# A relative-bias line stored 128 times, so that a strided transfer builds the strips without TensorE

## The chip, the cores and the metric

The kernel runs on one core of a Trainium2 chip. The metric is the device time of one execution in microseconds (us). The engines are TensorE (PE, with its weight loads as PEld), VectorE (DVE), ScalarE (ACT), GpSimd (POOL) and SyncE (SP), which here only issues DMA transfers.

## The reference, cut to what matters

Two model blocks in float32 run one after the other on 512 tokens of width 1024 (528 with 16 meta tokens in the first block). The first layer of the first block is the one that the change touches: a sparse attention with an index score that selects 128 keys for each query, and a relative-position bias for each head.

```
def rel_bucket(rel):            # rel = key position - query position; 32 buckets
    ...
def dsa_attention(q, k, v, iq, ik, iw, rel_bias, chunk, valid, topk):
    def block(i):               # 128 queries
        sc = relu(einsum('bqhd,bsd->bqhs', iqb, ik))
        score = einsum('bqhs,bqh->bqs', sc, iwb) * IDX_SCALE
        score = where(adm, score, NEG_INF)
        _, idx = lax.top_k(score, topk)
        logits = einsum('bqhd,bqkhd->bhqk', qb, kg) * dh ** -0.5
        bias = rel_bias[rel_bucket(idx - qpos)]
        logits = logits + transpose(bias)
        p = softmax(where(ok, logits, NEG_INF))
        return einsum('bhqk,bqkhd->bqhd', p, vg)
layer_ab: oa = dsa_attention(...) * silu(ag); ob = gla_chunked(...); out = concat(oa, ob) @ w_out
```

After it come a layer with retention and stick-breaking attention, and a second block with four feed-forward parts, a latent attention and a gated convolution.

## The kernel before

Activations stay in on-chip memory with the features on the partitions. All weights stream through in blocks of at most 1024 x 256 (1 MB): `load_block` (L436) asks for a block on SP's queue, `split_high` (L451, the activation at L459) rounds it on ACT to `wh`, `split_low` (L461, L466) makes the remainder `wl` on POOL, and PE makes three products for each tile (L486, L490 or L493, by form). There are two slots for a block: block b may be loaded when the low part of block b - 2 is made. The order on each engine is written out by hand in the five functions at the end (L2162 to L2341), and semaphores join them. PE's dense products are dealt out step by step between the small matmuls of attention stages.

The relative bias depends only on key minus query position, so the kernel makes one line for each head: a matmul of the bias table with a one-hot matrix gives `line`, 8 partitions (one for a head) x 655 values, which ACT copies out of PSUM (L2239, L2240). For 128 queries on the partitions the bias is then a strip: row p reads the line from position 127 - p on. SBUF rows can't be read at another offset for each partition, so the line goes to memory (`bias_line`, L2176) and comes back as `strip` (128 partitions x 8 heads x 528) with one transfer (L2181), in which row p starts at p. That is the wrong way round, and 16 matmuls with a reversed identity matrix (`flip`, `strips_pe`, L1641; the trace shows each as two) turn it, with 8 copies from PSUM on ACT (`strips_act`, L1647).

What stands around it:
- SP: store of the line, then the loads of further blocks, then the wait for the store (`bias_stored`) and for the end of the linear attention (`gla_mix_low`; the strips lie where its tiles lay), the transfer of the strips, the next blocks.
- ACT: `index_act` (L1504) begins with a wait for `bias_stored`, since `relu` lies where `line` lay. Ahead of it in ACT's order is the rounding of block 4. `index_act` makes the relu of the index scores (L1511) from matmuls at L1483; DVE adds them up (L1542, L1545). PE's first group of scores, two dense steps and the head weights (L1491) need no relu; every further group needs the relus of the group ahead of it.
- DVE then selects the keys by rounds of maximum and replace (L1586, L1587), the last ones alone before the softmax stage; L1589 and the memset at L1590 end each selection.
- The softmax stage (`soft_pe` L755, `soft_dve` L834, `soft_act` L898) has 40 steps of one head and one query tile: scores (L773), logits with bias (L852), maximum (L854), exponential (L910), turn (L785, L788), values (L804), and dense steps of the gate projection and the output projection as filling. In the first eight steps DVE reads `strip` itself (16 queries); from the ninth on POOL adds strip and selection mask ahead (L2208).

Of the kernel before, what the change touches and what calls it, by code (L numbers as in the profile page):

```python
# [5 lines left out]
F32 = mybir.dt.float32  # L6
# [3 lines left out]
ACT = mybir.ActivationFunctionType  # L10
AX = mybir.AxisListType

P = 128
# [4 lines left out]
T = SEQ + META  # L18
# [11 lines left out]
HEADS = 8  # L30
# [10 lines left out]
def token_tile(t):  # L41

    return (0, META) if t == 0 else (META + P * (t - 1), P)
# [54 lines left out]
BIAS_SPAN = T + P - 1  # L98
# [124 lines left out]
BLOCKS, FIRST, UNITS = weight_plan()  # L223


def units_before(b):
    return BLOCKS[b].unit0 if b < len(BLOCKS) else len(UNITS)


def evacs_before(b, engine):  # L230

    return sum(x[0] == engine for x in UNITS[:units_before(b)])
# [6 lines left out]
def program(nc, inp, const_in, buckets_in, out, bias_line):  # L239
# [3 lines left out]
    def S(name):  # L243

        if name not in sems:
            sems[name] = ctx.enter_context(nc.semaphore(name))
        return sems[name]


    ps = ctx.enter_context(nc.psum_tensor("ps", [P, 8, 512], F32))  # L250

    def at(name, off, shape, dtype=F32):

        assert off % 8 == 0
        return nc.alloc_sbuf_tensor_at(name, shape, dtype, offset=SBUF0 + 4 * off)
# [14 lines left out]
    def const(name, c0=0, n=None, rows=P):  # L270
        pack, at_, width = CONST[name]
        return K[pack][0:rows, at_ + c0:at_ + (width if n is None else c0 + n)]
# [9 lines left out]
    line = at("line", 33224, [HEADS, BIAS_SPAN])  # L282
# [35 lines left out]
    strip = at("strip", 37608, [P, HEADS, T])  # L318
# [102 lines left out]
    def banks(b0, width, rows=P):  # L421

        return ps[0:rows, b0:b0 + 2, 0:width // 2]

    def halves(ap, width):
        return ap.rearrange("p (a b) -> p a b", a=2) if len(ap.shape) == 2 else ap
# [968 lines left out]
    ag = [(AG + q, i) for q in range(2) for i in range(2)]  # L1395
# [34 lines left out]
    def dsa_between(eng, i):  # L1430

        for n, end in enumerate(DSA_ENDS):
# [3 lines left out]
            elif end == i - 1:  # L1436
                dsa_evict_dve(eng, n)

    dsa = Soft("dsa", [0, 1, 2, 3, 4],
               lambda h, c0, n: aqT[(h % 2) * HD:(h % 2) * HD + HD, h // 2, c0:c0 + n],  # L1440
               lambda h, c0, n: akT[(h % 2) * HD:(h % 2) * HD + HD, h // 2, c0:c0 + n],
               lambda kt, h: av[0:token_tile(kt)[1], kt, h * HD:(h + 1) * HD],
               lambda t: META + P * t, lambda t, n, h: rq[0:n, t:t + 1], None, 0, lg, pt, oa, mx, agT, 0, True, ((0,), (2,), 3, (4,), 7),
               None, dsa_between, oa_meta, lambda e: e.wait_ge(S("gate_silu"), 8))
# [20 lines left out]
    halfT = T // 2  # L1465
# [166 lines left out]
        nc.vector.scalar_tensor_tensor(out=halves(dst, T), in0=banks(bank_of(u), T, n), scalar=HD ** -0.5 if name == "bq" else 1.0,  # L1632
                                       in1=halves(rstd[0:n, :], T), op0=ALU.mult, op1=ALU.mult).then_inc(S("evac_dve"), 1)

    def strips_pe(pe):
        pe.wait_ge(S("side_in"), 32)
        for h in range(HEADS):
            if h >= 2:
                pe.wait_ge(S("strip_out"), h - 1)
            for x in range(2):  # L1640
                last = nc.tensor.matmul(ps[:, 2 + 2 * (h % 2) + x, 0:halfT], const("flip"), strip[:, h, x * halfT:(x + 1) * halfT], start=True, stop=True)  # L1641
            last.then_inc(S("strip_turned"), 1)

    def strips_act(act):
        for h in range(HEADS):
            act.wait_ge(S("strip_turned"), h + 1)
            nc.scalar.activation(halves(strip[:, h, :], T), banks(2 + 2 * (h % 2), T), ACT.Copy).then_inc(S("strip_out"), 1)  # L1647

    def cd_name(b):
        return [n for n in ("cq", "ck", "cv", "cg", "dk", "dq0", "dv0", "dg0", "dq1", "dv1", "dg1", "out_ret") if FIRST[n] <= b][-1]  # L1650

# [510 lines left out]
    @block.sync  # L2162
    def _(sp):
        sp.dma_start(xm[:, :], inp["meta_tokens"]).then_inc(S("const_in"), 16)
        sp.dma_start(K[0][:, :], const_in[0]).then_inc(S("const_in"), 16)
        load_block(sp, 0)
        for t in range(NT):
            sp.dma_start(xt[:, t, :], inp["x"][0, t * P:(t + 1) * P, :]).then_inc(S(f"x_in_{t}"), 16)
        load_block(sp, 1)
        sp.dma_start(onehot[:, :], buckets_in).then_inc(S("bias_in"), 16)  # L2170
        sp.dma_start(rb[:, :], inp["rel_bias"]).then_inc(S("bias_in"), 16)
        sp.dma_start(gate_w2[:, :], inp["gla_gate_w2"][0]).then_inc(S("side_in"), 16)
        for b in range(2, 4):
            load_block(sp, b)
        sp.wait_ge(S("bias_rows"), 2)
        sp.dma_start(bias_line, line[:, :]).then_inc(S("bias_stored"), 16)  # L2176
        for b in range(4, FIRST["ag"] + 1):
            load_block(sp, b)
        sp.wait_ge(S("bias_stored"), 16)
        sp.wait_ge(S("gla_mix_low"), NT + 1)  # L2180
        sp.dma_start(strip[:, :, :], bass.AP(bias_line.tensor, bias_line.offset, [[1, P], [BIAS_SPAN, HEADS], [1, T]])).then_inc(S("side_in"), 16)  # L2181
        for b in range(FIRST["ag"] + 1, C0 + 2):
            load_block(sp, b)
        sp.wait_ge(S("unit_done"), units_before(C0))
        sp.dma_start(K[1][:, :], const_in[1]).then_inc(S("side_in"), 16)
        sp.dma_start(K[3][:, :], const_in[3]).then_inc(S("side_in"), 16)
        for b in range(C0 + 2, FIRST["second"] + 2):
            load_block(sp, b)
        second_sp(sp)

    @block.gpsimd
    def _(pool):
        for b in range(OG + 1):
            split_low(pool, b)

        for i in range(HEADS, 5 * HEADS):
            t, h = dsa.steps[i]
            if i == HEADS:
                pool.wait_ge(S("strip_out"), HEADS)
            if h == 0:  # L2200
                pool.wait_ge(S("selected"), t)
            if i >= HEADS + 2:
                pool.wait_ge(S("dsa_logits"), i - 1)
            w = dsa.width(t)
            at_ = strip_at(t)
            if i == 3 * HEADS:
                pool.wait_ge(S("unit_done"), units_before(OG))
            nc.gpsimd.tensor_tensor(bm_of(i)[:, 0:w], strip[:, h, at_:at_ + w], score[:, SCO[t - 1]:SCO[t - 1] + w], ALU.add).then_inc(S("bias_masked"), 1)  # L2208
            if i in (9, 15, 23, 31):
                split_low(pool, OG + 1 + (9, 15, 23, 31).index(i))  # L2210
        for b in range(OG + 5, FIRST["second"]):
            split_low(pool, b)
        second_pool(pool)

    @block.scalar
    def _(act):
# [39 lines left out]
        lin_high(act, gla, NT)  # L2256
        for b, i in av_units[NT + 1:]:
            ab_act(act, b, i)
        strips_act(act)
        soft_act(act, dsa, lambda e: None)  # L2260
        for b in range(OG + 4, OG + 8):
            late_act(act, "cd", 2 * (b - OG - 4))
# [17 lines left out]
    def _(dve):  # L2280
# [37 lines left out]

        for _ in rounds:
            pass  # L2320
        soft_dve(dve, dsa, lambda e: e.wait_ge(S("strip_out"), HEADS))
        for b in range(OG + 4, OG + 8):
            add_out_dve(dve, b, True, "cd")
        late_scale_dve(dve, "cd")
# [17 lines left out]
    def _(pe):  # L2342
# [3 lines left out]
        for k in range(KT):  # L2346
            last = nc.tensor.transpose(ps[:, 4, k * META:(k + 1) * META], xm[:, k * P:(k + 1) * P], ident[0:META, 0:META])
# [3 lines left out]
        for g in range(2 * NT):  # L2351
# [8 lines left out]
            for k in range(4):  # L2360
                last = nc.tensor.transpose(ps[:, 4 + (g + 1) % 4, k * P:(k + 1) * P], xt[:, t, (k0 + k) * P:(k0 + k + 1) * P], ident)
# [35 lines left out]
        for _ in range(steps_in(av_units[NT + 1:])):  # L2397
            next(dense)
        pe.wait_ge(S("gla_gated"), NT + 1)
        strips_pe(pe)  # L2400
        pe.wait_ge(S("strip_out"), HEADS)

        def dsa_fill(i):
            if i == 6:
# [77 lines left out]
```

## Time and profile before

| | |
|---|---|
| median of the runs | 2760.39 us (2758.14 to 2762.59, 3 runs) |
| the profiled execution | 2754.39 us |
| its span, first to last instruction | 2752.6 us |
| mean granted clock of TensorE | 0.986 |
| PE / PEld busy | 95% / 78% |
| DVE / ACT / POOL busy | 38% / 32% / 39% |
| DMA, mean | 79 GB/s |

The profile is one execution. Busy shares are means over the whole span, in which many stages with different limits follow each other; the stages of this change are the first 300 us. A timeline row gives start, duration, engine, line, operation and tiles, and in brackets how long the engine was idle before it and what it waited for.

### The profile page before, as it was taken

The numbers are of one execution on the slowest core, as the hardware profiler recorded it, in microseconds if no ns is written. First come the engines' busy times: TensorE is split into PE (matmuls) and PEld (weight loads), VectorE is DVE, ScalarE is ACT, GpSimd is POOL, SyncE is SP. The second block draws the span as 40 slices with busy tenths as digits, with TensorE's granted clock in tenths as the row PEclk, the third lists the DMA queues.
The fourth block names the chain that finished last, engine by engine and source line by source line (L and its number), as shares of the span: only waits on it lengthen the run. The fifth ranks groups of instructions, "written<-read, shape, count | busy, mean of one in ns | idle before, by whom it ended". The sixth has DMA issues, their size and how long they took to land.

```text
span 2752.6 us, 32062 instructions
## 1 busy us (share of the span) xinstructions
PE 2623.4 (95%) x13245; PEld 2134.7 (78%) x13245; DVE 1033.9 (38%) x1742; ACT 881.1 (32%) x1289; POOL 1068.3 (39%) x830
## 2 busy tenths in 40 slices
PE   7999898999996999999789999999999999999999
PEld 6888787886655888877667888878888888888887
DVE  4655355224335312145554222243121444421212
ACT  4432333225543222232534222232222322322221
POOL 3232232331114444443204444444444444454443
PEclk9999999999998999999999999999999999999999
DMA  4122001220012233221102332233322232223322
GB/s 129 59 62 82 28 24 54 77 77 32 23 39 91 89 94 105 92 87 59 58 9 92 100 97 94 88 96 98 101 92 92 92 104 95 92 92 95 104 92 77
DMA packets 215851, 217.78 MB, mean 79 GB/s; under 512 B 10599, under 2 KB 213090, under 8 KB 215706
## 3 DMA queue, kind: packets, MB, share of 16 engines
q1 hardware_dynamic: 215504, 215.68, 24.5%
q8 instruction: 105, 1.72, 0.3%
q14 instruction: 40, 0.33, 0.0%
q10 hardware_dynamic: 202, 0.06, 0.0%
HBM read 213.60 MB, written 2.12 MB: 78 GB/s over the span
## 4 chain that ended last, share of the span: by engine, by line
PE 86%; DVE 5%; ACT 4%; issue 2%; POOL 2%; DMA 1%; ACTq 0%; DVEq 0%; SPq 0%
PE ps L490 65%; PE ps L486 7%; PE ps L493 3%; POOL wl L466 2%; PE ps L804 2%; PE ps L773 1%; ACT wh L459 1%; PE ps L2021 1%; PE ps L1999 1%; PE ps L788 1%; DVE score L1587 1%; PE ps L2415 1%; DVE top L1586 0%; PE ps L1483 0%; PE ps L1980 0%
## 5 line engine op out<-in xcount | busy, mean ns | idle before, releaser
L466 POOL TENSOR_TENSOR wl<-raw,wh 128x512 fp32r<-128x512 f32 x794 | 1039.6, 1340 | 1591.3 <-ACT wh L459 1591.3
L490 PE MATMUL ps<-NH,wh 128*128 128x512 f32 (+1 forms) x1824 | 720.8, 395 | 38.1 <-POOL wl L466 27.8
L490 PE MATMUL ps<-NL,wh 128*128 128x512 f32 (+1 forms) x1824 | 715.4, 392 | 0.0
L490 PE MATMUL ps<-NH,wl 128*128 128x512 f32 (+1 forms) x1824 | 714.8, 392 | 0.0
L459 ACT ACTIVATE wh<-raw 128x2048 fp32r<-128x2048 f32 (+4 forms) x219 | 380.3, 1737 | 459.9 <-PE ps L490 413.6
L490 PEld LDWEIGHTS ps<-NH,wh 128*128 128x128 f32 (+1 forms) x1824 | 344.9, 189 | 119.9 <-POOL wl L466 30.9
L490 PEld LDWEIGHTS ps<-NH,wl 128*128 128x128 f32 (+1 forms) x1824 | 344.7, 189 | 74.3
L490 PEld LDWEIGHTS ps<-NL,wh 128*128 128x128 f32 (+1 forms) x1824 | 344.9, 189 | 73.6 <-issue 1.4
L490 PE MATMUL ps<-GH,wh 128*128 128x512 f32 x832 | 330.0, 397 | 3.0 <-DVE GL L728 2.3
L490 PE MATMUL ps<-GH,wl 128*128 128x512 f32 x832 | 332.6, 400 | 0.0
L490 PE MATMUL ps<-GL,wh 128*128 128x512 f32 x832 | 329.1, 396 | 0.0
L986 DVE SCALAR_TENSOR_TENSOR H<-ps,H 128x512 f32<-128x512 f32 x96 | 66.4, 691 | 341.8 <-PE ps L490 341.8
L490 PEld LDWEIGHTS ps<-GH,wh 128*128 128x128 f32 x832 | 157.1, 189 | 41.0 <-issue 2.6
L490 PEld LDWEIGHTS ps<-GL,wh 128*128 128x128 f32 x832 | 157.1, 189 | 39.1
L490 PEld LDWEIGHTS ps<-GH,wl 128*128 128x128 f32 x832 | 156.9, 189 | 36.5
L953 ACT ACTIVATE GH<-tmp 128x512 fp32r<-128x512 f32 x88 | 55.7, 633 | 371.9 <-DVE tmp L979 371.9
L949 ACT ACTIVATE sg<-sg 128x512 f32<-128x512 f32 x88 | 55.7, 633 | 319.6 <-DVE sg L970 319.6
L970 DVE TENSOR_TENSOR sg<-ps,rstd 128x512 f32<-128x512 f32 x66 | 45.6, 692 | 236.7 <-PE ps L490 236.6
L976 DVE TENSOR_TENSOR tmp<-ps,rstd 128x512 f32<-128x512 f32 x66 | 45.7, 692 | 211.9 <-PE ps L490 211.9
L486 PE MATMUL ps<-NH,wh 128*128 128x264 f32 (+1 forms) x448 | 96.5, 297 | 10.0 <-ACT aqT L1607 4.0
L981 DVE TENSOR_TENSOR GL<-tmp,GH 128x512 fp32r<-128x512 f32 x88 | 73.6, 836 | 61.6 <-ACT GH L953 61.6
L493 PE MATMUL ps<-wh,NH 128*128 128x256 f32 (+1 forms) x320 | 90.8, 284 | 2.1 <-ACT bv L1614 2.1
(389 smaller groups left out, 3074.7 us busy)
## 6 DMA issues: line engine op xcount, KB each, us to landing
raw<-in_ffn_w_gate SPq DMA_DIRECT2D x44, 1024.0 KB, 5.3
raw<-in_ffn_w_up SPq DMA_DIRECT2D x44, 1024.0 KB, 5.3
raw<-in_ffn_w_down SPq DMA_DIRECT2D x32, 1024.0 KB, 4.9
raw<-in_w_in_ab SPq DMA_DIRECT2D x16, 1024.0 KB, 5.6
raw<-in_w_in_cd SPq DMA_DIRECT2D x14, 1024.0 KB, 5.0
raw<-in_ffn_w_down SPq DMA_DIRECT2D x16, 768.0 KB, 4.2
raw<-in_c_w_in SPq DMA_DIRECT2D x12, 1024.0 KB, 5.0
raw<-in_w_out_ab SPq DMA_DIRECT2D x8, 512.0 KB, 3.5
```

What stands on the lines that cost most here:

```text
L459: nc.scalar.activation(wh[:, b % 2, 0:k, 0:w], raw[:, b % 2, 0:k, 0:w], ACT.Copy).then_inc(S("weights_high"), 1)
L466: ins = nc.gpsimd.tensor_tensor(wl[:, b % 2, ks, 0:w], raw[:, b % 2, ks, 0:w], wh[:, b % 2, ks, 0:w].bitcast(F32), ALU.subtract)
L486: last = nc.tensor.matmul(ps[0:m1 - m0, bank + h, 0:T // 2], w[:, s, k, m0:m1], x(k)[:, h * (T // 2):(h + 1) * (T // 2)], start=start, sto ...
L490: last = nc.tensor.matmul(ps[0:m1 - m0, bank, 0:SEQ], w[:, s, k, m0:m1], x(k), start=start, stop=stop)
L493: last = nc.tensor.matmul(ps[0:n_tok, bank, 0:total], x(k)[:, c0:c0 + n_tok], w[:, s, k, 0:total], start=start, stop=stop)
L804: last = nc.tensor.matmul(ps[0:n, A.value_at[i % len(A.value_at)], 256:256 + HD], A.pt[0:kn, i % 2, a0:a0 + n], A.v(kt, h), start=(x == 0) ...
L949: nc.scalar.activation(sg[:, i, :], sg[:, i, :], ACT.Silu).then_inc(S("gate_silu"), 1)
L953: nc.scalar.activation(GH[:, 2 * p_ + i, :], tmp[:, i, 0:SEQ], ACT.Copy).then_inc(S("hidden_high"), 1)
L970: nc.vector.tensor_tensor(sg[:, i, :], ps[:, bank_of(u + i), :], r, ALU.mult).then_inc(S("evac_dve"), 1)
L976: nc.vector.tensor_tensor(tmp[:, i, 0:SEQ], ps[:, bank_of(u + 2 + i), :], r, ALU.mult).then_inc(S("evac_dve"), 1)
L981: nc.vector.tensor_tensor(GL[:, 2 * p_ + i, :], tmp[:, i, 0:SEQ], GH[:, 2 * p_ + i, :].bitcast(F32), ALU.subtract).then_inc(S("hidden_low" ...
L986: nc.vector.scalar_tensor_tensor(out=H[:, m, META:T], in0=ps[:, bank_of(u), :], scalar=0.5, in1=H[:, m, META:T], op0=ALU.mult, op1=ALU.add ...
```

## The change

The line is written to memory 128 times for each head, so `bias_line` is 8 x 128 x 655. The store has a source that repeats each of its 8 rows 128 times. The transfer of the strips reads copy p of a head from position 127 - p on: 127 into the tensor, and then 654 further for each partition. So the strips arrive in final order. `strips_pe` and `strips_act` are gone, and those who waited for them wait for the transfer (`side_in` at 32). PE, which waited for ACT's copies before the first scores, now waits for ACT's last copy of the value projection. All other code is as before.

```diff
-    def strips_pe(pe):
-        pe.wait_ge(S("side_in"), 32)
-        for h in range(HEADS):
-            if h >= 2:
-                pe.wait_ge(S("strip_out"), h - 1)
-            for x in range(2):
-                last = nc.tensor.matmul(ps[:, 2 + 2 * (h % 2) + x, 0:halfT], const("flip"), strip[:, h, x * halfT:(x + 1) * halfT], start=True, stop=True)
-            last.then_inc(S("strip_turned"), 1)
-
-    def strips_act(act):
-        for h in range(HEADS):
-            act.wait_ge(S("strip_turned"), h + 1)
-            nc.scalar.activation(halves(strip[:, h, :], T), banks(2 + 2 * (h % 2), T), ACT.Copy).then_inc(S("strip_out"), 1)
-
...
         sp.wait_ge(S("bias_rows"), 2)
-        sp.dma_start(bias_line, line[:, :]).then_inc(S("bias_stored"), 16)
+        sp.dma_start(bias_line, line[:, :].rearrange("h (a s) -> h a s", a=1).broadcast_to([HEADS, P, BIAS_SPAN])).then_inc(S("bias_stored"), 16)
         for b in range(4, FIRST["ag"] + 1):
             load_block(sp, b)
         sp.wait_ge(S("bias_stored"), 16)
         sp.wait_ge(S("gla_mix_low"), NT + 1)
-        sp.dma_start(strip[:, :, :], bass.AP(bias_line.tensor, bias_line.offset, [[1, P], [BIAS_SPAN, HEADS], [1, T]])).then_inc(S("side_in"), 16)
+        sp.dma_start(strip[:, :, :], bass.AP(bias_line.tensor, bias_line.offset + P - 1, [[BIAS_SPAN - 1, P], [P * BIAS_SPAN, HEADS], [1, T]])).then_inc(S("side_in"), 16)
...
-                pool.wait_ge(S("strip_out"), HEADS)
+                pool.wait_ge(S("side_in"), 32)
...
-        strips_act(act)
         soft_act(act, dsa, lambda e: None)
...
-        soft_dve(dve, dsa, lambda e: e.wait_ge(S("strip_out"), HEADS))
+        soft_dve(dve, dsa, lambda e: e.wait_ge(S("side_in"), 32))
...
-        strips_pe(pe)
-        pe.wait_ge(S("strip_out"), HEADS)
+        pe.wait_ge(S("evac_act"), evacs_before(FIRST["ag"], "A"))
...
-    bias_line = nc.dram_tensor("bias_line", (HEADS, BIAS_SPAN), F32, kind="Internal").ap()
+    bias_line = nc.dram_tensor("bias_line", (HEADS, P, BIAS_SPAN), F32, kind="Internal").ap()
```

How instructions stand on ACT between the value projection and the first exponential, before:

```order
L1614 ACTIVATE av<-ps,rtok 128x256 [waits parts_ready,unit_done] x4
L459 ACTIVATE wh<-raw 128x2048 [waits unit_done,raw_ready_0]
L1647 ACTIVATE strip<-ps 128x528 [waits strip_turned] x8
L910 ACT_TABLE_LOAD
L910 ACTIVATE lg,mx<-lg,mx 16x16 [waits dsa_max] x2
```

and after, where the eight copies are gone and the table load, which waits for nothing, stands right behind the rounding of a block:

```order
L1614 ACTIVATE av<-ps,rtok 128x256 [waits parts_ready,unit_done] x4
L459 ACTIVATE wh<-raw 128x2048 [waits unit_done,raw_ready_0]
L910 ACT_TABLE_LOAD
L910 ACTIVATE lg,mx<-lg,mx 16x16 [waits dsa_max] x2
L910 ACTIVATE lg,mx<-lg,mx 16x16 [waits dsa_values_out,dsa_max]
```

SP's queue around the store, after; only the store's own row has changed (it was `8x655`), and what stands behind it is in the same places:

```order
L444 DMA raw<-in_w_in_ab 128x8x256 [waits weights_low]
L2162 DMA bias_line<-line 1024x1x655 [waits bias_rows]
L444 DMA raw<-in_w_in_ab 128x8x256 [waits weights_low] x12
L2167 DMA strip<-bias_line 128x8x528 [waits gla_mix_low,bias_stored]
L444 DMA raw<-in_w_in_ab 128x8x256 [waits weights_low]
```

## Rows read from the trace of the kernel before

**Rows 1.** The page: busy time of each engine, and the chain that ended last.

```profile
PE 2623.4 (95%) x13245; PEld 2134.7 (78%) x13245; DVE 1033.9 (38%) x1742; ACT 881.1 (32%) x1289; POOL 1068.3 (39%) x830
...
PE 86%; DVE 5%; ACT 4%; issue 2%; POOL 2%; DMA 1%; ACTq 0%; DVEq 0%; SPq 0%
```

**Rows 2.** Timeline around the turn of the strips: start, duration (us), engine, operation.

```profile
274.13 1.94 PE L1641 MATMUL ps<-strip,K 128*128 128x264 f32 x8
278.18 5.76 PE L1641 MATMUL ps<-strip,K 128*128 128x264 f32 x24 [2.10 <-ACT strip L1647]
...
274.33 0.47 ACT L1614 ACTIVATE av<-ps,rtok 128x256 f32<-128x256 f32 x1 [2.37 <-PE ps L493]
...
283.98 0.61 ACT L1647 ACTIVATE strip<-ps 128x528 f32<-128x528 f32 x1 [0.28 <-PE ps L1641]
```

**Rows 3.** Timeline of the first softmax step.

```profile
283.03 0.11 DVE L1590 MEMSET score<- 64x64 f32 x1
...
284.60 1.28 ACT L910 ACT_TABLE_LOAD   x1
...
285.01 0.22 DVE L852 SCALAR_TENSOR_TENSOR lg<-ps,rq,strip 16x16 f32<-16x16 f32 x1 [1.86 <-PE ps L773]
285.27 0.16 DVE L854 TENSOR_REDUCE mx<-lg 16x1 f32<-16x16 f32 x1
...
285.90 0.31 ACT L910 ACTIVATE lg<-lg,mx 16x16 f32<-16x16 f32 x1
...
286.46 0.51 PE L486 MATMUL ps<-NH,wh 128*128 128x264 f32 x2
```

**Rows 4.** SP's issues, then DMA packets in 35.4:36.4, 35.8:36.2 and 45:52 us.

```profile
35.07 0.34 SPq L2176 DMA_DIRECT2D bias_line<-line  x1
45.48 8.03 SPq L444 DMA_DIRECT2D raw<-in_w_in_ab  x2
...
DMA packets 16, 0.02 MB, mean 21 GB/s; under 512 B 8, under 2 KB 8, under 8 KB 16
...
q1 hardware_dynamic: 16, 0.02, 12.5%
...
DMA packets 13, 0.02 MB, mean 52 GB/s; under 512 B 5, under 2 KB 5, under 8 KB 13
...
DMA packets 1040, 1.05 MB, mean 150 GB/s; under 512 B 16, under 2 KB 1040, under 8 KB 1040
```

**Rows 5.** Timeline of ACT and PE where the index scores begin.

```profile
59.44 1.91 ACT L459 ACTIVATE wh<-raw 128x2048 fp32r<-128x2048 f32 x1 [9.44 <-PE ps L486]
61.26 0.45 ACT L1511 ACTIVATE relu<-ps 128x144 f32<-128x144 f32 x2
...
61.53 1.05 PE L1491 MATMUL ps<-K,baw 8*128 8x8 f32 x8
63.30 0.67 PE L1483 MATMUL ps<-ikT,iqT 64*128 64x72 f32 x8 [0.72 <-DVE iw L1533]
```

**Rows 6.** Stretches: length, PE, PEld, DVE, ACT, POOL busy, granted clock, DMA share, GB/s.

```profile
287.00:290.60 3.60, 3.60 (x19) 3.60 (x18) 0.00 (x0) 0.00 (x0) 0.00 (x0) 0.53 0.00 0
290.60:294.00 3.40, 3.40 (x29) 3.28 (x27) 0.00 (x0) 0.00 (x0) 0.00 (x0) 1.00 0.00 0
```

**Rows 7.** The strip load: issue, time to landing (last column), rate, the block behind.

```profile
264.09 0.37 SPq L2181 DMA_DIRECT2D strip<-bias_line  x1
...
strip<-bias_line SPq DMA_DIRECT2D x1, 2112.0 KB, 8.3
raw<-in_w_in_ab SPq DMA_DIRECT2D x1, 1024.0 KB, 11.2
...
265.50:272.50 7.00, 7.00 (x62) 7.00 (x61) 6.69 (x15) 1.42 (x3) 2.15 (x2) 1.00 1.00 343
...
275.71 1.91 ACT L459 ACTIVATE wh<-raw 128x2048 fp32r<-128x2048 f32 x1 [0.91 <-DMA raw<-in_w_in_ab]
```

**Rows 8.** Packets of the store in 35.80:35.85 and in 36.0:36.05 us.

```profile
q1 hardware_dynamic: 3, 0.01, 103.0%
...
q1 hardware_dynamic: 1, 0.00, 17.6%
```

## The prediction

> **What bounds the kernel now.** I read the page first: TensorE (PE) is busy for 95% of the span, and the chain that ended last runs through it for 86% [rows 1]. Any time in which PE stands still in a stage that nothing overlaps is therefore paid in full, and any PE work that is taken away is a gain only if no other engine ends later. The change touches two such stages, so I read the timeline of each, and the DMA view of the transfers between.
>
> The stage with the strips: PE ends the value projection at about 274.3 us. Then it turns the strips, 8 + 24 matmuls from 274.13 to 283.94 with a wait of 2.10 us inside, while ScalarE (ACT) copies them out, the last one from 283.98 [rows 2]. The first real softmax step follows. What matters is what VectorE (DVE) does meanwhile: it is still selecting the top keys, and its last instruction of that is the memset at 283.03, which ends at 283.14 [rows 3]. DVE can't touch the first logits before that, strips or no strips.
>
> The stage near the start: the bias line (8 rows of 2620 bytes) is stored at 35.07, the next weight block is asked for on the same queue at 45.48 [rows 4], ACT rounds that block at 59.44, and only then makes the first relu of the index scores, at 61.26 [rows 5]. That relu also waits until the store has landed.
>
> **Part 1: the turn goes.** 32 matmuls and 8 copies leave the program. Before, the first exponential started at 285.90 because the table load at 284.60 (1.28 us) could start only behind ACT's last strip copy; the logits and their maximum were ready at 285.43 [rows 3]. After the change, ACT has nothing ahead of the table load but the rounding of a weight block, over before 278, so the table is in place early: the load at 284.60 ran before the maximum existed, so it waits for nothing. The first step then hangs on DVE alone: free at 283.14, logits 0.22 and maximum 0.16 in the same spacing as before (285.01 to 285.43, 0.42 us) give 283.56; exponential and turn as before (285.90 to the first dense matmul at 286.46, 0.56 us) give 284.1. The dense matmuls that follow are PE's, one after the other, and started at 286.46. **Gain 2.3 us**, not the 9.9 us of the strips, since the selection on DVE becomes what is late.
>
> The new wait of PE at this place, for the last copy of the value projection, is over at about 274.8 and has only the first scores behind it. PE stands idle for some 9 us instead of turning. The granted clock already fell behind the turn: 0.53 in 287.0 to 290.6, 1.00 after it [rows 6]. The stretch cost 3.6 x (1 - 0.53) = 1.7 us and I take that it comes again, no better and no worse; if the idle time brings a second such stretch the gain is 0.6 us, if the fall moves into the idle time it is 4.0 us. The bias additions on GpSimd, which read the strips too, begin only at the ninth step and move along with the steps.
>
> **Part 2: the strided load.** It has the shape it had, 128 x 8 runs of 2112 bytes, landed in 8.3 us, at 272.4 [rows 7]. Its readers now wait for DVE until 283.1, so there are 10.7 us of cover. The weight block behind it landed at 275.7, where ACT begins to round it [rows 7]; PE comes to that block only after the 16 dense steps of the block ahead of it, which begin at 286.46 [rows 3]. It costs nothing on the path.
>
> **Part 3: the store in 128 copies.** This decides. It writes 8 x 128 rows of 2620 bytes, 2.68 MB, where it wrote 0.02 MB. The trace doesn't show such a store, so I bound it from both sides.
> - Fast end: the rate of the strip load, 343 GB/s with all engines busy [rows 7], gives 2.68 / 0.343 = 7.8 us. But the store of before has 16 packets, 8 of them under 512 bytes, where a weight block of 1024 runs has 1040, 16 of them under 512 bytes [rows 4]. I read the small ones as one closing packet for each DMA engine, so 8 engines served the 8 rows. The source still starts with the 8 rows. At 343 / 16 = 21.4 GB/s for an engine the 128 rows of each take 128 x 2620 / 21.4 = 15.7 us.
> - Slow end: the same 8 rows of before. In 35.8 to 36.2 us the transfer moved its 8 data packets, 52 GB/s [rows 4]. 2.68 / 0.052 = 51.6 us. That a packet is slow because others read beside it is in the finer windows: three that began together took 1.03 x 16 x 50 / 3 = 275 ns each, one alone 0.176 x 16 x 50 = 141 ns [rows 8]. With the mean of all, 0.125 x 16 x 1000 / 8 = 250 ns, it is 32 us.
> All three kinds of figure are for 8 packets at the start of a transfer, when an engine has also to begin; a stream could be faster. I take 51 us, since the new store repeats exactly this pattern, 8 partitions read at once, and its crowded packets are those slower by half or more.
>
> The Trainium skill, "DMA: Bandwidth & Descriptors", in "Why a DMA increments its semaphore by 16 and not by 1", says that the slowest dimension of both sides sets the number of engines, at most 16: 8 here, as the packet count shows, and by it alone the store would take the 15.7 us. "SBUF — State Buffer", in "Door 1: The DMA port swizzle", puts partitions 0 to 3 on one port and 4 to 7 on another, each of 27.2 GB/s: the estimate by that page is 2.68 / 0.0544 = 49 us. It speaks against the change, and the 52 GB/s of [rows 4] agree with it as far as 8 packets can.
>
> Who waits. The data start at 35.8, so the store lands at 35.8 + 51 = 86.8. The weight block asked for at 45.48 stands behind it in the same queue. How that goes is seen at the strips: the block behind them took 11.2 us to land and came at 275.7, 3.3 us after the strips [rows 7]. So this one lands at 90.1 instead of before 59. ACT's order is rounding of this block (1.91 us with 0.09 overlap, hence + 1.8), then relu: 91.9 instead of 61.26. PE's next scores need the first two relus (0.45 us): 92.5 instead of 63.30 [rows 5]. PE, DVE and GpSimd have nothing else to do: PE's dense steps of this stage are dealt out between the scores, the selection needs the scores complete, and all later stages follow from here. **Cost 92.5 - 63.3 = 29.2 us.** Behind a PE idle from 62.6 [rows 5] for 30 us I add one slow stretch, 1.7 us [rows 6].
>
> **The sum**: + 29.2 + 1.7 - 2.3 = + 28.6 us. The profiled execution took 2754.4 us, 1.8 of it outside its span of 2752.6; it would be 2783. The median of the runs shown is 2760.4, 6 us above the profiled one, and the forecast is for such a median: 2789 us.
>
> **Rivals.**
> - The store is no slower than its engines (15.7 us or less). It lands by 51.5, the block behind it by 54.8, ACT wants it at 59.44: hidden entirely. Then only part 1 counts, 2760.4 - 2.3 = 2758 us, not slower. For it: a lone packet of 2620 bytes took 141 ns, 128 of which are 18 us, and the cover lasts until a store of some 20 us (35.8 + 20 + 3.3 = 59.1). Against it: the crowded packets. Chance 0.19. It decides at those 20 us; above them each microsecond of the store is one of the kernel.
> - The packets keep the mean of 250 ns, 32 us: landing 67.8, block 71.1, relu 72.9, scores 73.5, + 10.2 + 1.7 - 2.3 = + 9.6, 2770 us. With all stores of 25 to 45 us, 0.14.
> - Every packet of a crowd costs more than its share, because each engine reads one row at a time and the stream never evens out: 62 us, landing 97.8, scores at 103.5, + 40.2 + 1.7 - 2.3, 2800 us. Chance 0.05.
> - That PE gains the whole 9.9 us of the turn: it would need DVE to be free at 275, and it isn't [rows 3]. Chance 0.01, and it would have to come on top of a hidden store: 2751 us.
> - The forecast itself, stores of 45 to 60 us: 0.61.
>
> **How the numbers follow.** Slower by over 0.2% (5.5 us, about what a measurement tells from no change) are the forecast, the slow rival and nearly all of the middle one: 0.79. Within 0.2% is the hidden store, since 2.3 to 4 us are less than that, and the edge of the middle rival: 0.18. Faster is left with 0.03, the whole gain of the turn and what could lie above 5.5 us of a hidden store. The range leaves out the hidden store and starts with the middle rival's edge: 25 us of store give 35.8 + 25 + 3.3 + 1.8 + 0.6 = 66.5, + 3.2 + 1.7 - 2.3, 2763 us. It ends with the slow rival's 2800 and a further clock stretch or two, 2804 us.
>
> **What would show it.** In the profile of after: the landing of the store near 87 us, DMA near 52 GB/s from 36 to 87 us, PE idle from about 62 to 92 with ACT idle for the weight block, the first relu near 92; then the top-key selection ending the wait of the first logits, no strip rows on PE, and the first dense matmul of the softmax stage 1 us behind the end of the selection. If the first relu is at 61 as before, part 3 is wrong; if it comes at the landing itself, the block wasn't held up behind the store and 5 us less are lost. If the span up to the selection's end has not grown but the whole has, something I don't see is at work.

## The result, and the profile after

The changed kernel took 2802.2 us as the median of 4 runs (2788.2 to 2817.5), the kernel before 2761.5 us beside it (4 runs): ratio 1.0148, 95% interval 1.0112 to 1.0183. It is slower, as forecast; the median lies 13 us above the forecast's 2789 us and inside its range of 2763 to 2804 us, 2 us below the upper end. The profiled execution took 2788.96 us, its span 2787.2, against 2754.39 and 2752.6 before: + 34.6 us. The profiled execution of the kernel before was a fast one, 7 us below the median of 2761.5; from that median to 2788.96 it is 27.5 us.

The page of after: busy times as before, but for 32 matmuls on PE and 8 copies on ACT [rows 1]; and the chain that ended last, now with more DMA.

```profile
PE 2622.6 (94%) x13213; PEld 2134.3 (77%) x13213; DVE 1033.9 (37%) x1742; ACT 876.5 (31%) x1281; POOL 1069.0 (38%) x830
...
PE 84%; DVE 6%; ACT 4%; issue 2%; DMA 2%; POOL 2%; ACTq 0%; DVEq 0%; SPq 0%
```

The timeline of after where the index scores begin, SP, ACT and PE in turn (start, duration, ..., in brackets the idle time before and what ended it), and one piece of the chain (start, duration, what):

```profile
35.06 0.86 SPq L2162 DMA_DIRECT2D bias_line<-line  x1
45.46 0.38 SPq L444 DMA_DIRECT2D raw<-in_w_in_ab  x1
...
93.40 1.91 ACT L459 ACTIVATE wh<-raw 128x2048 fp32r<-128x2048 f32 x1 [43.41 <-DMA raw<-in_w_in_ab]
95.22 0.45 ACT L1511 ACTIVATE relu<-ps 128x144 f32<-128x144 f32 x2
...
95.81 1.13 PE L1483 MATMUL ps<-ikT,iqT 64*128 64x72 f32 x8 [33.25 <-ACT relu L1511]
...
45.46 47.91 DMA raw<-in_w_in_ab
```

ACT waits 43.41 us for the weight block that was asked for behind the store, then rounds it and makes the first relu, at 95.22 instead of 61.26 [rows 5]; PE waits 33.25 us for that relu. The windows of after over the same time (columns as in [rows 6]; the last three are clock, DMA share, GB/s) tell how the two transfers ran:

```profile
44.00:48.00 4.00, 4.00 (x26) 3.32 (x25) 0.00 (x0) 3.01 (x4) 1.44 (x2) 1.00 0.63 81
48.00:52.00 4.00, 4.00 (x35) 4.00 (x34) 1.91 (x3) 1.97 (x4) 3.96 (x4) 1.00 0.75 151
70.00:80.00 10.00, 0.00 (x0) 0.00 (x0) 0.00 (x0) 0.00 (x0) 0.00 (x0) 0.50 0.48 50
90.00:94.00 4.00, 0.00 (x0) 0.00 (x0) 0.00 (x0) 0.60 (x1) 0.00 (x0) 0.50 0.52 186
```

The store goes on at 50 GB/s with half of the 16 engines busy. Its packets of 2620 bytes run in the trace from 36.5 to 90.3 us. What was moved above those 50 GB/s from 44 to 52 us is 4 x (81 - 50) + 4 x (151 - 50) = 530 KB, half of the weight block of 1024 KB, and only that block was asked for then: it is the half that fell to the idle engines. The other half starts when the store ends, at 90.3, and is done at 93.4. From the DMA share, 8 engines moved 50 GB/s at 0.48 of 16, so a packet of 2620 bytes took 0.48 x 16 x 2620 / 50000 = 0.40 us.

The first softmax step of after, and the stretches at half and at full clock behind it:

```profile
311.40 1.28 ACT L910 ACT_TABLE_LOAD   x1
...
317.21 0.11 DVE L1590 MEMSET score<- 64x64 f32 x1
317.26 0.22 DVE L852 SCALAR_TENSOR_TENSOR lg<-ps,rq,strip 16x16 f32<-16x16 f32 x1
317.54 0.28 PE L773 MATMUL ps<-akT,aqT 64*16 64x8 f32 x4 [8.15 <-DVE lg L852]
317.71 0.31 ACT L910 ACTIVATE lg<-lg,mx 16x16 f32<-16x16 f32 x1 [5.03 <-DVE mx L854]
318.28 0.81 PE L486 MATMUL ps<-NH,wh 128*128 128x264 f32 x2
...
318.30:321.30 3.00, 3.00 (x14) 3.00 (x14) 0.23 (x2) 0.40 (x2) 0.00 (x0) 0.50 0.38 126
321.30:325.00 3.70, 3.70 (x31) 3.70 (x31) 0.00 (x0) 0.00 (x0) 0.00 (x0) 0.97 0.00 0
```

No strip rows are left; the table load stands long before the exponential; the first logits follow the memset at once, and the first dense matmul comes 0.96 us behind its end (317.32), where it was 3.32 us before [rows 3]. PE is idle for 8.15 us where it had turned the strips.

One thing about single runs is needed for the medians below: some runs of nearly every kernel here, the kernel before included, take 15 to 27 us more than the rest.

### The profile page after: what moved, and what is told of

It is laid out like the page before. It is cut to its first block, busy times and chain, and to the rows that moved or that the text cites. A ratio compares the mean times of both kernels' runs of the same rounds, so it can differ in the third digit from the quotient of the medians.

```text
span 2787.2 us, 31990 instructions
## 1 busy us (share of the span) xinstructions
PE 2622.6 (94%) x13213; PEld 2134.3 (77%) x13213; DVE 1033.9 (37%) x1742; ACT 876.5 (31%) x1281; POOL 1069.0 (38%) x830
## 4 chain that ended last, share of the span: by engine, by line
PE 84%; DVE 6%; ACT 4%; issue 2%; DMA 2%; POOL 2%; ACTq 0%; DVEq 0%; SPq 0%
PE ps L490 64%; PE ps L486 6%; PE ps L493 3%; POOL wl L466 2%; DMA raw<-in_w_in_ab 2%; PE ps L804 2%; PE ps L773 1%; ACT wh L459 1%; PE ps L2007 1%; DVE score L1587 1%; DVE top L1586 1%; PE ps L1985 1%; PE ps L788 1%; PE ps L2399 1%; PE ps L1483 0%
## 5 line engine op out<-in xcount | busy, mean ns | idle before, releaser
L490 PEld LDWEIGHTS ps<-GH,wl 128*128 128x128 f32 x832 | 156.9, 189 | 36.5
L486 PE MATMUL ps<-NL,wh 128*128 128x264 f32 (+1 forms) x448 | 92.8, 289 | 0.0
```

The lines of the kernel that those rows point to most:

```text
L486: last = nc.tensor.matmul(ps[0:m1 - m0, bank + h, 0:T // 2], w[:, s, k, m0:m1], x(k)[:, h * (T // 2):(h + 1) * (T // 2)], start=start, sto ...
L490: last = nc.tensor.matmul(ps[0:m1 - m0, bank, 0:SEQ], w[:, s, k, m0:m1], x(k), start=start, stop=stop)
```

## The experiments

The ratios are to runs of the kernel before on the same chip in the same session; they are not the ratios of the medians, and a few high runs can raise them. In the kernels with an added line the later line numbers are one higher (L1512 is the relu, L774 the scores).

**The store alone.** The kernel before with only its store changed to 128 copies; the strips are read from copy 0 and still turned. Edit, with COPIES = 128:

```
-sp.dma_start(bias_line, line[:, :])
+sp.dma_start(bias_line, line[:, :].rearrange("h (a s) -> h a s", a=1).broadcast_to([HEADS, COPIES, BIAS_SPAN]))
-... [[1, P], [BIAS_SPAN, HEADS], [1, T]]
+... [[1, P], [COPIES * BIAS_SPAN, HEADS], [1, T]]
```

> The kernel before, with the store in 128 copies as its only edit: the strips are read from copy 0 and still turned on TensorE. My theory (the store costs all, the turn's removal gives a little back): the weight block lands near 93, the first relu at 95.2 as in the changed kernel, and the selection ends 34 us later than before; the time is 34 to 36 us above before, 2 to 3 us above the changed kernel. Rival (the loss comes from the idle TensorE where the turn stood, or from the strided load): within 0.2% of before.

Measured: 2797.7 us (4 runs), ratio 1.0136 (1.0115 to 1.0158). ACT's rows:

```profile
92.94 1.91 ACT L460 ACTIVATE wh<-raw 128x2048 fp32r<-128x2048 f32 x1 [43.42 <-DMA raw<-in_w_in_ab]
94.75 0.45 ACT L1512 ACTIVATE relu<-ps 128x144 f32<-128x144 f32 x2
```

The same wait, and a loss at least as large, with the turn and the old load of the strips kept: it is the store's. It is larger than I expected, 37.0 us for 34 to 36, and 5.8 us above the changed kernel in the same session (2791.9, below) where I had said 2 to 3. The turn accounts for 2.4 of these (the first dense matmul again comes 3.32 us behind the memset, 325.88 - 322.56); the rest is at least in part clock. Behind PE's idle stretch the half clock lasted longer than in the profile of after; the same window in the store alone, then in after:

```profile
99.00:104.00 5.00, 5.00 (x28) 4.39 (x29) 1.92 (x3) 0.47 (x2) 1.02 (x1) 0.50 0.57 167
```
```profile
99.00:104.00 5.00, 5.00 (x44) 4.53 (x43) 3.02 (x6) 0.95 (x4) 1.48 (x2) 0.94 0.46 115
```

With COPIES = 64:

> The kernel before with the store in 64 copies (half the bytes) as its only edit; the strips are still turned. Theory (50 GB/s whatever the size, and everything above a store of some 20 us is lost): the store takes 27 us and ends by 63, the block lands at 66.5, the first relu is at 68.2 instead of 61.3, and the time is 6 to 8 us above before: a fifth of the loss for half the bytes. Rival (loss in proportion to the bytes): 17 us.

Measured: 2782.3 us (10 runs: five of 2765.9 to 2773.4, five of 2791.3 to 2798.7), ratio 1.0061 (1.0021 to 1.0100), the first relu at 70.94.

```profile
52.00:56.00 4.00, 4.00 (x35) 3.91 (x35) 3.63 (x4) 0.00 (x0) 2.15 (x2) 1.00 0.47 49
...
69.12 1.91 ACT L460 ACTIVATE wh<-raw 128x2048 fp32r<-128x2048 f32 x1 [18.09 <-DMA raw<-in_w_in_ab]
```

The rate is the same with half the copies, so the time is one of packets, not of a fixed wait. 64 copies fewer brought the relu 23.8 us nearer (94.75 to 70.94), 0.37 us for each. It came 2.7 us later than I expected (68.2): the store took the 27 us that I expected, but ran from 37.6 to 64.5 and not until 63, and the block landed 4.6 us behind it and not 3.5. Why the block took longer here isn't settled. The time missed by more: I expected 6 to 8 us, and even the five low runs are 4 to 11 us above the median of before (2762.2), the median of all ten 20.1. In the trace the selection ends 13.1 us later than before (296.27 for 283.14), 8.2 of them from the late scores (71.54 for 63.30) and 4.9 from half clock behind PE's idle time. The rival of a loss in proportion to the bytes (17 us) is refuted by the relu, which came 9.7 us late for 34 in after, and not by the run times.

**The same bytes from other partitions.** Three kernels like the changed one (128 copies, strided load, no turn), in which the line stands on more partitions: the bias table is repeated along its columns by GpSimd (`rbw`), so that the same two matmuls give the line on 32, 128 or 16 partitions. The stores:

```
spread8:  line[0:32:4] -> 128 copies each      8 rows, on partitions 0, 4, ..., 28
spread16: line[0:128] -> 8 copies each         16 rows of each head
spread2:  line[0:16] -> 64 copies each         2 neighbouring rows of each head
```

> The changed kernel with each head's line made on 4 partitions (the bias table is widened by one small copy on GpSimd), and stored from partitions 0, 4, ... 28: still 8 rows, 128 copies, 8 DMA engines, same bytes, but rows four partitions apart. Theory (rows of neighbouring partitions share a path of some 26 GB/s, four at a time): packets of 100 to 125 ns instead of 398, the store done in 13 to 17 us, by 52; first relu at 61.3 and the whole time at or 2.4 us below before. Rival (8 engines that repeat a row are slow in themselves, or writes of this kind to memory are): 50 GB/s and the time of the changed kernel, 34 us above before in the profile.

> The changed kernel with each head's line made on 16 partitions, so that all 128 hold a line, and each is stored in 8 copies: same bytes and same result in memory, 16 DMA engines. Theory: 340 GB/s or so, the store done in 8 to 9 us, by 45, before the next weight block is asked for; first relu at 61.3, the first dense matmul of the softmax stage at 284.1 against 286.5 before, time 1 to 4 us below before (0.1%), not clear of noise. Rival (writes to memory are what is slow, whatever the source): 50 GB/s again, 34 us above before.

> The changed kernel with each head's line on 2 neighbouring partitions, 16 in all, stored 64 times from each: same bytes, 16 rows and so 16 DMA engines, which is more engines than in the run from partitions 0, 4, ... 28, but again four neighbours to a path, now four paths. Theory (four neighbouring partitions share some 26 GB/s): 100 to 105 GB/s, 26 us, end by 62, first relu at 67 to 68, time 2 to 6 us above before. Rival (the number of engines decides): 340 GB/s, end by 44, first relu at 61.5, time as before.

Measured: spread8 2760.1 us (10 runs), ratio 1.0008 (0.9987 to 1.0028), relu at 61.73. spread16 2760.4 us (10 runs), ratio 0.9996 (0.9967 to 1.0026), relu at 61.83. spread2 2769.0 us (10 runs), ratio 1.0024 (0.9992 to 1.0055), relu at 70.62. Windows within the store, of spread8, spread16 and spread2:

```profile
38.00:41.00 3.00, 3.00 (x15) 2.43 (x14) 0.00 (x0) 1.11 (x3) 0.00 (x0) 1.00 0.52 202
```
```profile
36.50:41.00 4.50, 4.50 (x21) 3.68 (x20) 0.00 (x0) 1.01 (x2) 0.00 (x0) 1.00 0.92 361
```
```profile
52.00:60.00 8.00, 8.00 (x68) 7.64 (x67) 3.48 (x4) 0.00 (x0) 2.00 (x2) 1.00 0.95 100
64.00:68.00 4.00, 0.00 (x0) 0.00 (x0) 0.14 (x2) 0.00 (x0) 0.00 (x0) 0.86 1.08 366
```

The same 2.68 MB take 54 us from 8 neighbouring partitions, 14 from 8 that are four apart (190 GB/s), 27 from 16 neighbours, 7 from 128. The number of engines isn't it: spread8 keeps 8 engines (share 0.52) and is nearly four times as fast, spread2 has 16 busy engines (share 0.95) and only doubles. Nor are the writes to memory, which are the same in all. Each four neighbouring partitions gave 25 GB/s: 50 for 8, 100 for 16; and one row in each four, in spread8, gave about as much, 190 / 8 = 24. In the forecast the page "SBUF — State Buffer" of the Trainium skill ("Door 1: The DMA port swizzle") stood for this, and the trace agrees: one path to memory for four neighbours, 25 GB/s measured. The relu of spread2 is 3 us later than I expected (67 to 68): its store ran from 37.3 to 64.3 and not until 62, and the block landed 4.5 us behind it. All 16 engines were in the store (100 GB/s until it ended), so none of the weight block went ahead; but in the store of 64 copies, where half had gone ahead, the block landed as long behind, so this isn't shown to be what made it late. The time of spread2, 6.8 us above before in the medians, isn't clear of noise.

**The other queue.** The changed kernel with the store issued from ACT's queue, so that the weight block doesn't stand behind it on SP's:

```
-sp.wait_ge(S("bias_rows"), 2); sp.dma_start(bias_line, ...)
+act.wait_ge(S("bias_rows"), 2); act.dma_start(bias_line, ...)
```

> The changed kernel with the store issued from ScalarE's queue instead of SyncE's, right behind its two copies of the line. The weight block of 45.5 us then stands in another queue than the store, but both queues are served by the same DMA engines. Theory A (the block waited only because it stood behind the store in one queue): it lands long before the store's end, the first relu waits for the store alone, at 90 us instead of 95.2, and 5 us come back. Rival B (an engine that is busy with crowded rows is late for every queue): the block lands near 93 as before, relu near 95, nothing comes back. In both the time stays 28 us or more above before: the relu waits for the store in any case.

Measured: 2816.2 us (4 runs: 2790.4 and three of 2816 to 2817), ratio 1.0165 (1.0100 to 1.0230).

```profile
60.00:84.00 24.00, 2.82 (x24) 2.51 (x22) 0.95 (x5) 0.00 (x0) 0.00 (x0) 0.62 0.50 67
...
89.59 1.91 ACT L459 ACTIVATE wh<-raw 128x2048 fp32r<-128x2048 f32 x1 [39.35 <-DMA raw<-in_w_in_ab]
91.44 0.47 ACT L1511 ACTIVATE relu<-ps 128x144 f32<-128x144 f32 x2
```

The theory of the queue fell: the block landed at 89.59, 3.8 us earlier, and not long before the store's end. From 60 on the two run side by side, 67 GB/s together, and end nearly together, the store's last packets at 91. An engine that is busy with the crowded rows is late for both queues. The relu came at 91.44, between theory A (90) and rival B (95); the 3.8 us that it gained don't show in the run times, whose one low run (2790.4) is as long as the low ones of the changed kernel.

**What the turn is worth.** The forecast says that the selection on DVE hides all but 2.3 us of it. A cut of the selection for the last tile to 8 of its 16 rounds (64 keys in place of 128, so that tile's mask differs) lifts that cover, in the kernel before and in spread16:

```
-for n in range(TOPK // 8):
+for n in range(TOPK // 16 if j == NT - 1 else TOPK // 8):
```

> The kernel before with the selection for the last query tile cut to 8 of its 16 rounds (so 64 keys instead of 128 for those queries; that part of the computation is left out). VectorE is free some 12 us earlier, by 271. Theory (the turn of the strips holds the first softmax step by itself as well, through the strips and ACT's table load): the first logits stay at 285.0 and the first dense matmul of the stage at 286.5, give or take 0.5 us. Rival (VectorE's selection alone held it): both move up by several us.

> The kernel whose store is spread over all 128 partitions and that has no turn, with the selection for the last query tile cut to 8 of its 16 rounds (64 keys instead of 128 for those queries; that part is left out). Theory (with the turn gone the selection was what was late, and behind it ACT): VectorE free by 272; the first exponential then follows the last copy of the value projection, the rounding of a weight block and the table load, near 279, and the first dense matmul of the stage is at 279.5 to 281, 6 to 7 us ahead of the cut kernel with the turn. Rival (something else holds the first step at 286): no gain against the cut kernel with the turn, or 2.4 us as in the whole one.

Measured, one run each: short_before 2757.9 us, short_spread 2751.3. Rows of short_before, then of short_spread:

```profile
270.43 0.11 DVE L1591 MEMSET score<- 64x64 f32 x1
...
286.29 0.51 PE L486 MATMUL ps<-NH,wh 128*128 128x264 f32 x2
```
```profile
270.80 0.11 DVE L1592 MEMSET score<- 64x64 f32 x1
...
275.49 0.22 DVE L853 SCALAR_TENSOR_TENSOR lg<-ps,rq,strip 16x16 f32<-16x16 f32 x1 [4.58 <-PE ps L774]
277.46 1.28 ACT L911 ACT_TABLE_LOAD   x1
279.33 0.81 PE L487 MATMUL ps<-NH,wh 128*128 128x264 f32 x2
```

With the turn, a selection 12.6 us shorter moves the dense matmuls by 0.2 us; without it, they come at 279.33, 7.0 us earlier. So the turn and the selection each hold the first step to about the same time, and with the turn gone the selection is what holds it, as forecast (spread16, with the whole selection, has these matmuls at 286.15); with both away, the rounding of a block and the table load on ACT are next (277.46).

**spread16 again**, on another chip:

> The kernel with the line on 128 partitions, stored 8 times from each, and without the turn, once more against before with more rounds, since its traces show the first softmax step 2.4 us sooner after the end of the selection (0.97 against 3.3 us). Theory: 0.1% faster, at the edge of what can be told. Rival: the small copy and the wider line cost as much as is won, and the clock's stretches cover both: ratio 1.000 with an interval across it.

Measured: 2760.1 us (12 runs), ratio 1.0019 (0.9991 to 1.0046); the median is 2.4 us below before, and 4 of the 12 runs were of 2776 to 2787. So with the store repaired, the turn's removal is worth nothing that 10 or 12 runs can tell.

**After again**, in the session of the store alone:

> The changed kernel once more, to see its runs beside before on this chip. Two of its four runs took 2815 to 2818 us at a mean granted clock of 0.965 to 0.966, two 2788 to 2789 at 0.977. If the 27 us belong to the change, some of these runs show them again while those of before stay within 5 us; if they belong to the chip or the moment, before shows such runs as well or the changed kernel shows none.

Measured: 2791.9 us (6 runs, 2789.2 to 2815.0), ratio 1.0111 (1.0087 to 1.0135). Two of the 6 were high (2810.6, 2815.0), and 2 of the 19 of before beside them (2775.0, 2781.4), so such runs belong neither to the change alone nor to one session.

**Filling the gap.** The 8 dense steps that fill the first softmax step go ahead of PE's wait for the gated operand, in spread16 and in the kernel before:

```
+for _ in range(DSA_KSTEPS[0]):
+    next(dense)
 pe.wait_ge(S("gla_gated"), NT + 1)
...
-for _ in range(DSA_KSTEPS[i]):
+for _ in range(DSA_KSTEPS[i] if i else 0):
```

> Kernel: the one with the line stored from 128 partitions (spread16), and the 8 dense steps that filled TensorE's wait of softmax step 0 are done straight behind the value projection, before TensorE waits for the gated operand; step 0 then has no fill. Question: is TensorE's idle stretch of about 8 us behind the last selection's TensorE work worth its length once something is put in it? Theory: yes. The 8 dense steps are 48 matmul pairs that took from 286.5 to about 294 in the kernel before; the idle stretch begins at about 274.3, so they end at about 281 there, before the first logits are wanted, and what stood in their place at 286 (softmax step 1's own work) comes 7 to 8 us earlier. Expected: TensorE's idle stretch shrinks from 8.2 us to 1 to 3 us, span 2749 to 2752 us, median 7 to 9 us below the kernel before, ratio 0.997. Rival: the softmax steps behind it wait for VectorE's and ScalarE's work (the first logits, the exponentials), which starts no earlier; then step 1 finds TensorE idle again, for up to the 7.5 us that were taken away, and the median stays at the kernel before's, ratio 1.000.

> Kernel: the one before, turn on TensorE kept, with the same edit: the 8 dense steps of softmax step 0 straight behind the value projection, none in step 0. Theory: the dense steps take about 274.3 to 281, the turn's matmuls then start at once instead of in the idle stretch, so its last copy comes at about 288.6 instead of 283, the table load and the first exponentials come 4 to 5 us later than in the kernel before (exp at about 290), and of the 7.5 us saved 3 to 4 are left: median 3 to 4 us below the kernel before, ratio 0.9987. Rival as for the other kernel: nothing is saved, and with the exponentials later the time is up to 5 us above the kernel before, ratio 1.000 to 1.002. Together the two tell what the turn's removal is worth when TensorE's idle stretch beside it is filled: by the theory 4 to 5 us, against the 0.3 to 0.5 us that it gave in the kernel with the turn removed alone.

In the second one the first unit of the gate projection stands in PSUM banks 5 and 6, and the turn writes bank 5 as well, so half of that unit is replaced in what this kernel computes. Instructions and shapes are those of the edit, so the time can be read; but the edit isn't open to the kernel with the turn without another bank.

Measured: prefill_spread 2754.7 us (12 runs), ratio 0.9976 (0.9956 to 0.9996). prefill_before 2759.6 us (12 runs), ratio 1.0001 (0.9965 to 1.0036). Rows of prefill_spread, then of prefill_before:

```profile
283.33 0.11 DVE L1591 MEMSET score<- 64x64 f32 x1
...
283.66 0.26 PE L774 MATMUL ps<-akT,aqT 64*16 64x8 f32 x4 [3.03 <-DVE lg L853]
...
294.34 0.26 PE L774 MATMUL ps<-akT,aqT 64*16 64x8 f32 x4
```
```profile
283.73 0.11 DVE L1590 MEMSET score<- 64x64 f32 x1
...
288.54 1.28 ACT L910 ACT_TABLE_LOAD   x1
...
300.72 0.26 PE L773 MATMUL ps<-akT,aqT 64*16 64x8 f32 x4
```

The last row of each is the scores of the fourth softmax step. Counted from the end of the memset they come after 10.9 us in prefill_spread, 16.9 in prefill_before, 17.1 in spread16 repeated (302.73 - 285.63) and 18.4 in the kernel before (301.56 - 283.14). So in these traces the turn costs 1.3 us where PE idles anyway, and 6.0 us where that time is used; in the medians of the two prefill kernels it is 4.9 (expected 4 to 5). Of the 7 to 9 us that I expected of prefill_spread it gave 7.2. prefill_before gave 2.3 and not 3 to 4 in the medians, and 1.5 in the trace; its interval doesn't tell that from nothing. Of the 7.5 us that I wanted to save, some were slow clock, and they came back in the next fill: at full clock the 48 matmuls of the 8 steps took 5.9 us (274.4 to 280.3), and the next 48 took 8.4 us at a mean clock of 0.68 in prefill_spread (285.94 to 294.3), 8.8 at 0.65 in prefill_before (291.94 to 300.7).

prefill_spread is faster than the kernel before, by a quarter of a per cent, and the interval just leaves out no change. It was not run beside spread16 or the changed kernel.

## Why the prediction was right, and by how much each step missed

- **The rate of the store**: taken 52 GB/s and 51 us, from 8 packets that began together. Measured 50 GB/s from 36.5 to 90.3 us, 53.8 us. The choice among the rows (the crowded packets, not their mean of 250 ns nor the strip load's 343 GB/s) was the right one, and its reason too: neighbouring partitions share a path, as spread8 and spread2 show. My remark that a stream could be faster than a start was wrong, it kept the 0.40 us a packet that 52 GB/s for 8 of them mean (8 x 2620 / 52000).
- **The block behind**: 3.3 us behind the store, measured 3.1 (90.3 to 93.4). The size was right, but its reason, the queue, was half of it: half the block had been moved at 48 to 52 by the idle engines, and on another queue the block gained 3.8 us of 34.
- **Who waits**: ACT, relu, scores as said; 93.4, 95.22, 95.81 for 90.1, 91.9, 92.5. All three are 3.3 us late: 2.8 for the store's length and 0.7 for its start (36.5 for 35.8), less 0.2 for the block. The scores came 32.5 us later than before, for a forecast of 29.2.
- **The slow stretch behind PE's idle time**: + 1.7. From the first scores to the end of the selection after takes 317.32 - 95.81 = 221.5 us, before 283.14 - 63.30 = 219.8: + 1.7. That it is the forecast's number is luck. The same stretch took 224.8 us in after repeated (+ 5.0), 227.2 with the store alone (+ 7.4), 224.7 with 64 copies (+ 4.9), 224.8 with the store on ACT's queue (+ 5.0) and 223.9 in spread2 (+ 4.1); it took 221.3 in spread8 and spread16 (+ 1.5), where the relu was on time. So of the six profiles with a late relu five lost 4 to 7 us here, and the term was sized too small for them.
- **The turn**: gain 2.3 us. Measured 3.32 - 0.96 = 2.4 at the first dense matmul, and 2.4 still at the fourth step's scores (333.30 - 317.32 against 18.42). That part of it can be lost to the clock again was named in the forecast and shows in spread16: 3.5 us of dense matmuls at 0.50 from 286.5 on, and 1.3 us left of 2.4.
- **The sum**: 32.5 + 1.7 - 2.4 = + 31.8 up to the softmax stage, forecast 28.6. The span grew by 34.6. The sum missed by 3.2 us, all of it the store's lateness. The other 2.8 us of the span lie behind 866 us, in more time at half clock around the next stage, where 59 us of the same work (equal counts on DVE, ACT and POOL) were granted a mean of 0.82 instead of 0.88; the windows of before, then of after:

```profile
834.50:893.50 59.00, 40.08 (x157) 31.12 (x156) 30.14 (x33) 21.63 (x25) 25.44 (x18) 0.88 0.27 85
```
```profile
866.00:925.00 59.00, 41.32 (x151) 31.96 (x150) 30.14 (x33) 21.63 (x25) 25.44 (x18) 0.82 0.27 84
```

  The change doesn't make them. The same stretch (the same counts on DVE, ACT and POOL) ran at 0.88 in the changed kernel repeated, as in before, and at 0.82 in short_before, which has the old store and the turn; the windows of these two:

```profile
890.78:949.78 59.00, 40.05 (x157) 31.11 (x156) 30.14 (x33) 21.64 (x25) 25.41 (x18) 0.88 0.28 85
```
```profile
834.91:893.91 59.00, 41.40 (x150) 31.89 (x149) 30.13 (x33) 21.63 (x25) 25.39 (x18) 0.82 0.27 85
```

  So they differ from one execution to the next, and the profile of before happened to be a fast one.
- **The median** is 13 us above the forecast, and this was in no step: 2 of the 4 runs were at 2788 to 2789, 2 at 2815 to 2818. That the lower ones meet the forecast's 2789 is in part luck: the forecast put 6 us on the profiled execution, since that of before was 6 us below its median, and the profiled execution of after, 2788.96, is 6 us above the 2783 that the forecast gives for it. I read the higher ones as a long stretch at half clock in the softmax stage, which a profiled run of 2810.6 us (after repeated) and one of 2816 us (the store on ACT's queue, 415 to 476 us at a mean of 0.52) show and the profiles of the other kernels don't; the higher runs of the first measurement were not themselves profiled. Windows of after repeated:

```profile
405.00:420.00 15.00, 14.66 (x98) 11.97 (x97) 6.97 (x23) 5.48 (x16) 6.34 (x6) 1.00 0.12 36
420.00:440.00 20.00, 19.51 (x77) 15.72 (x76) 8.28 (x20) 3.92 (x10) 4.12 (x4) 0.55 0.00 0
440.00:468.00 28.00, 28.00 (x104) 22.97 (x104) 8.63 (x25) 6.59 (x16) 7.39 (x6) 0.50 0.06 20
```

  Such runs aren't the change's alone: the kernel before had 11 of 2774 to 2787 us in the 78 runs beside the experiments. With a slow store they were more frequent, 7 in 14 for the changed kernel and its twin on ACT's queue and 5 in 10 for the store of 64 copies, but 0 in 4 for the store alone with 128. Whether such a store makes them more frequent, and what starts the long stretch, stays open.
- **The rivals**: the hidden store (15.7 us) exists, but for other partitions: spread8, with a store of 14 us, is that rival, 2760.1 us. It gave no measurable gain, as its 2.3 us said. The others (stores of 25 to 45 us, of 62 us, the whole turn as a gain) didn't come; the last showed its condition in short_spread, DVE free early.

## What to carry over

Before one row is written many times, look at how many partitions it is read from and how far apart these lie: 8 neighbours gave 50 GB/s, the same 8 rows four apart 190. A transfer is paid through whatever shares its engines behind it, on whichever queue, so count its cover up to the first reader of the next one. And taking work off the busiest engine pays little while another engine holds the same step, unless other work fills the hole: here the turn of 9.9 us was worth 1.3 to 2.4 us by itself, 5 to 6 with the fill moved in.

## What the runs showed of the hardware that I had not expected

- A stream of packets from 8 neighbouring partitions ran at 50 GB/s, 0.40 us a packet, no faster than the first eight; 16 neighbours on 16 engines at 100 GB/s, 8 rows four apart at 190, 128 partitions at 361.
- Half of a weight block overtook a store that had been issued 10 us earlier on the same queue (151 GB/s in 48 to 52), and the other half waited 40 us for it.
- SP's own issue of the block after that one took 30.8 us, for 0.37 at the median, while the store was running in its queue (the longest of the 21 in the row below; minimum, median and maximum in ns). With 64 copies the longest was 3.8 us, with the store on ACT's queue 1.05. Nothing here shows that it cost time.

```profile
L444 SPq DMA_DIRECT2D raw<-in_w_in_ab x21: 368/368/30775, 1.6 to 298.7; - x21
```

- The table load for the exponential ran when ACT was free and not when the data were there: 311.40 for an exponential at 317.71.
- TensorE was granted half its clock (1.2 GHz of 2.4) from 420 to 468 us in after repeated, in the last 28 of them busy 28.00 us, behind a stretch busy 14.66 of 15 us at full clock. Unlike the half clock at 66 to 99 us in after, it had hardly any idle time ahead of it.
